# Making the low part of streamed weights for two halves of a block by one instruction

## The reference, cut to what matters

```python
def sqrelu_mlp(h, w_up, w_down):
    u = jax.nn.relu(h @ w_up)
    return (u * u) @ w_down

def reference(x, ...):
    for layer in range(DEPTH):                       # DEPTH = 2
        h = rmsnorm(x, norm_mix_w[layer])
        y = hybrid_mixer(h, ...) if layer % 2 == 0 else swa_sink_attention(h, ...)
        x = x + y
        h = rmsnorm(x, norm_mlp_w[layer])
        x = x + sqrelu_mlp(h, mlp_w_up[layer], mlp_w_down[layer])
    return rmsnorm(x, final_norm_w)
```

## Time and profile before

| what | value |
|---|---|
| median of three runs | 2006.84 us (2005.88 to 2007.82) |
| profiled execution, its span from the first to the last instruction | 2005.7 us |
| TensorE busy | 1997.1 us, 9161 products |
| VectorE busy | 1450.5 us, 2028 instructions |
| ScalarE busy | 1027.4 us, 1360 instructions |
| low parts on VectorE (L854) | 708 of 128x1024, 858.9 us |
| transfers of weights on SyncE's queue | 57.0% of the 16 engines' span |

### The profile page before, as it was taken

How to read it: one execution, slowest core, us unless ns; L and a number is a source line. 1 busy time by engine, 2 the same in 40 slices (tenths; PEclk the granted TensorE clock), 3 DMA queues, 4 the chain that set the end, 5 groups by cost and what they waited for, 6 DMA issues and landing times.

```text
span 2005.7 us, 24710 instructions
## 1 busy us (share of the span) xinstructions
PE 1997.1 (100%) x9161; PEld 1653.1 (82%) x9161; DVE 1450.5 (72%) x2028; ACT 1027.4 (51%) x1360; POOL 45.1 (2%) x55
## 2 busy tenths in 40 slices
PE   9999999999999999999999999999999999999998
PEld 8888888888888888888888878888888888888887
DVE  6777778987558647755889887988548756854875
ACT  6665665455345435434545566555435444534554
POOL 1110110000000000000000000000000000000000
PEclk9999999999999999999999999999999999999999
DMA  8556546556555565555655544565565555565563
GB/s 304 181 176 214 170 167 211 189 189 209 191 189 192 198 195 185 193 195 181 210 189 189 169 162 163 181 203 194 194 197 193 192 190 187 187 209 189 189 201 113
DMA packets 191756, 382.48 MB, mean 191 GB/s; under 512 B 6328, under 2 KB 7616, under 8 KB 191552
## 3 DMA queue, kind: packets, MB, share of 16 engines
q1 hardware_dynamic: 190288, 377.51, 57.0%
q0 software_dynamic: 1216, 3.88, 0.6%
q10 hardware_dynamic: 176, 0.07, 0.0%
HBM read 379.34 MB, written 2.10 MB: 190 GB/s over the span
## 4 chain that ended last, share of the span: by engine, by line
PE 98%; DVE 1%; issue 0%; ACT 0%; DMA 0%; ACTq 0%
PE acc L1215 31%; PE acc L1217 31%; PE acc L1216 31%; DVE area L1052 1%; PE bank L1305 0%; PE bank L1382 0%; PE bank L1406 0%; PE bank L1392 0%; DVE w_lo L854 0%; PE acc L1244 0%; PE acc L1248 0%; PE acc L1252 0%; PE bank L1347 0%; PE bank L1336 0%; PE bank L1337 0%
## 5 line engine op out<-in xcount | busy, mean ns | idle before, releaser
L854 DVE TENSOR_TENSOR w_lo<-raw,w_hi 128x1024 fp32r<-128x1024 f32 x708 | 858.9, 1223 | 497.8 <-ACT w_hi L622 494.9
L622 ACT ACTIVATE w_hi<-raw 128x1024 fp32r<-128x1024 f32 x708 | 743.5, 1060 | 772.3 <-PE acc L1217 771.0
L1215 PE MATMUL acc<-w_hi,a_hi 128*128 128x512 f32 x1552 | 607.1, 391 | 0.0
L1217 PE MATMUL acc<-w_hi,a_lo 128*128 128x512 f32 x1552 | 604.1, 389 | 0.0
L1216 PE MATMUL acc<-w_lo,a_hi 128*128 128x512 f32 x1552 | 604.0, 389 | 0.0
L1215 PE MATMUL acc<-w_hi,b_hi 128*128 128x512 f32 x1264 | 492.3, 389 | 0.0
L1216 PE MATMUL acc<-w_lo,b_hi 128*128 128x512 f32 x1264 | 491.8, 389 | 0.0
L1217 PE MATMUL acc<-w_hi,b_lo 128*128 128x512 f32 x1264 | 491.7, 389 | 0.0
L1215 PEld LDWEIGHTS acc<-w_hi,a_hi 128*128 128x128 f32 x1552 | 291.4, 188 | 61.2 <-issue 0.9
L1217 PEld LDWEIGHTS acc<-w_hi,a_lo 128*128 128x128 f32 x1552 | 291.3, 188 | 60.9
L1216 PEld LDWEIGHTS acc<-w_lo,a_hi 128*128 128x128 f32 x1552 | 291.4, 188 | 60.0
(11 more groups left out here) (204 smaller groups left out, 602.1 us busy)
## 6 DMA issues: line engine op xcount, KB each, us to landing
raw<-in_mlp_w_up SPq DMA_DIRECT2D x128, 1024.0 KB, 5.3
raw<-in_mlp_w_down SPq DMA_DIRECT2D x128, 1024.0 KB, 5.1
raw<-in_hyb_w_in SPq DMA_DIRECT2D x44, 1024.0 KB, 5.2
raw<-in_attn_w_qkv SPq DMA_DIRECT2D x20, 1024.0 KB, 5.2
raw<-in_hyb_w_out SPq DMA_DIRECT2D x16, 1024.0 KB, 5.1
raw<-in_attn_w_out SPq DMA_DIRECT2D x16, 1024.0 KB, 5.0
raw<-in_hyb_w_in SPq DMA_DIRECT2D x5, 512.0 KB, 9.5
out_y<-x SPq DMA_DIRECT2D x4, 512.0 KB, 3.0
```

Of the source, the lines that this page charges most:

```text
L622: nc.scalar.activation(w_hi[:, h % RING], raw[:, h // 2, 2 * (h % 2):2 * (h % 2) + 2, :], ACT.Copy).then_inc(hi_ready, 1)
L854: nc.vector.tensor_tensor(w_lo[:, h % RING], raw[:, h // 2, 2 * (h % 2):2 * (h % 2) + 2, :], w_hi[:, h % RING].bitcast(F32), ALU.subtract) ...
L1215: nc.tensor.matmul(a, xh, wh, start=first, stop=False)
L1217: ins = nc.tensor.matmul(a, xl, wh, start=False, stop=last)
```

## The change

`cut_lo` does nothing at an even half. At an odd half it waits for that half's high part, which comes after that of the even half, and makes the low parts of both by one instruction over 128x2048 elements; the semaphore rises by 2. The raw weights of the two halves lie side by side in one place, and their two places of the ring too.

```diff
@@ cut_lo, on VectorE @@
                 h = n % HALVES
                 if slot.b * HALVES + n >= NBLK * HALVES:
                     return
+                if h % 2 == 0:
+                    return
+                to = slice(h % RING - 1, h % RING + 1)
                 dve.wait_ge(hi_ready, slot.halves(n + 1))
-                nc.vector.tensor_tensor(w_lo[:, h % RING], raw[:, h // 2, 2 * (h % 2):2 * (h % 2) + 2, :],
-                                        w_hi[:, h % RING].bitcast(F32), ALU.subtract).then_inc(lo_ready, 1)
+                nc.vector.tensor_tensor(w_lo[:, to].rearrange("p h e n -> p (h e) n"), raw[:, h // 2],
+                                        w_hi[:, to].rearrange("p h e n -> p (h e) n").bitcast(F32),
+                                        ALU.subtract).then_inc(lo_ready, 2)
```

## The result

The changed kernel takes 2098.88 us (median of four runs, 2098.01 to 2100.95) against 2007.07 us of the kernel before in the same session: 1.0462 times as long, with a 95% interval of 1.0447 to 1.0477. The forecast was 2079 us; the time lies 0.9 us above the top of the range.

What follows compares the result with a forecast made beforehand. TensorE, busy 1997.1 of 2005.7 us, was taken to bound the kernel. Waits at the listed places summed to 72.0 us, making the span 2077.7; with the median 1.1 higher, the forecast was 2079 us, range 2050 to 2098.

Steps and rivals of the forecast that it cites:

- TensorE bounds the kernel: Whole kernel: TensorE busy 1997.1 of 2005.7 us, so savings on other engines bring at most 8.6 us.
- The price of the long instruction: Each low part of 128x2048 on VectorE: 2.29 us, with bounds of 1.23 and 2.46.
- The places: Waits placed behind `up`, `res`, `q`, `k`, `aq`, `v`, `g`, in slots 55 and 56, at start and end: 72.0 us.
- the ring sets the earliest start of a pair: Any pair: its high part starts only after half k-3; with nothing else to do, ready 3.58 us later, due at 5.44.
- No waits behind `down`: Slots behind `down`: no TensorE waits at pairs expected; seeing some would be a sign of being wrong.
- What a wait costs beyond its length: Every TensorE wait: 0.17 us added for restart, signal and load, with bounds of 0 and 0.31.
- the lateness of the pair: Behind `up` and similar, 36 places: pair ends at 11.30 against 10.88 us, late by 0.42.
- TensorE's clock falls: Behind six waits of 3 to 5 us: nine products at 1.2 GHz pace, 1.8 us each wait; 2090 us, chance 0.10.
- a granted clock under full after the long waits: TensorE after long waits: a profile sign that the forecast is wrong; no size given.
- Waits breed waits: Even pairs with slack run late because a late pair delays loads and evacuations: above 2098 us, chance 0.08.
- Behind `v`: Decay of retention scores stands behind the pair 5.4/5.5: 1.43 us late with the restart, twice.
- half 56.0: One slot after slot 55: what is late there is late again, 1.55 us.

Runs made afterwards that it cites:

- the ring of eight: Changed kernel with rings of high and low parts holding eight halves instead of four, two low-part buffers left out: 2036.47 us, ratio 1.0155.
- the pairs first: Changed kernel with each pair placed on VectorE ahead of the odd tick's own work instead of behind it: 2219.42 us, ratio 1.1062.

## Why the prediction was wrong by 20 us

**Right.** That TensorE bounds the kernel and VectorE's saving is worth nothing (shown by the pairs behind `down`). The Trainium skill (VectorE: DVE Perf Modes, the section on the TRN2 errata) advises large tiles to pay the fixed latency less often; the trace agrees on VectorE, busy 43.7 us less, and the kernel's time rose all the same. The price of the long instruction, 2.294 us against 2.29. The places, and what stands ahead of each: four transposes, twelve, two pairs against 10.88 us. That the ring sets the earliest start of a pair, from which that arithmetic begins, is shown by the ring of eight. No waits behind `down` appeared.

**The step that failed: "What a wait costs beyond its length".** It gave each wait 0.17 and let everything go on at 0.227 us a product from there. Behind the long waits and at the start TensorE did not go on at that pace: 14.2 us, most of the miss, and the next part is on them. Behind the short waits the term was nearly right in its sum, and not in its parts. It was made of 0.08 from the earlier trace rows and of 0.09 for signal and load, which no row shows. And that row isn't one of a restart: a small product runs just ahead of half 0.6, which starts at 28.65 (TensorE's timeline in the kernel before):

```profile
28.56 0.28 PE L1471 MATMUL bank<-ident,vec_rows 72*128 72x72 f32 x1
```

In the change, 51 of the 58 waits have no slow half behind them. In 38 of these the half begins 0.05 behind the pair's end and takes 0.14 longer in the mean; in the other 13 it begins 0.15 behind and takes 0.08 longer. That is 0.20 for 0.17, some 2 us in all.

**A second term was too small: the lateness of the pair.** Behind `up` the pair ends 0.52 late, not 0.42: 36 times 0.10, 3.5 us. That the late start came out at 0.57 for 0.58 is luck, 0.10 more here against 0.12 less in the signal. Of the 0.10, 0.07 lies between a high part's end and its low part's start, for which the sum had 0.03. That holds in the kernel before (ScalarE, then VectorE, in slot 19):

```profile
454.44 1.06 ACT L622 ACTIVATE w_hi<-raw 128x1024 fp32r<-128x1024 f32 x1
455.53 1.23 DVE L854 TENSOR_TENSOR w_lo<-raw,w_hi 128x1024 fp32r<-128x1024 f32 x1 [1.92 <-ACT w_hi L622]
```

There the low part starts 0.03 behind the high part's end, as in all 382 cases in which VectorE had been idle for over 0.1 us; the pair in slot 19 starts 0.10 behind it (507.18 + 1.06, then 508.34), as do 243 of 245 such pairs. With two instructions it is 0.03 again. Whether the length makes it, the signal of 2 or something else, was not tried.

**The rival that was put aside came true: "TensorE's clock falls".** It had 0.10, because TensorE would be idle "but a few us at a time, between long stretches of work". That argument has no row behind it, and it is wrong; the prediction had named a granted clock under full after the long waits as a sign of being wrong, and that sign came. Behind each of the six waits of 3.3 to 4.8 us in the changed kernel, and behind that of 1.71 at the start, a half ran slow, with the granted clock at or near half in the windows. They cost 1.73 + 2.31 + 1.52 + 1.72 in slots 3, 4, 9 and 10, 2.66 + 1.30 at the start and 2.57 + 0.40 in slot 55, 14.2 us together. The rival assumed nine products, or 1.8 us each, at six places, 11 us: the right size. The added products show that idleness is the cause at the four places where they stood. The Trainium skill (TensorE: Matmul & The Clock Gate, section HAM oscillation) describes this for waits on data; the trace agrees here for waits on another engine.

**"Waits breed waits"** has its number, above 2098, by 0.9 us, but not its mechanism: slots with slack, those behind `down`, run as before.

**Sizes.** Behind `v` 2.02 was measured for 1.43. Of the 0.6, 0.42 is the pair 5.4/5.5 itself. The timeline of VectorE, then of GpSimd:

```profile
156.56 2.71 DVE L857 TENSOR_TENSOR w_lo<-raw,w_hi 128x2048 fp32r<-128x2048 f32 x1 [1.50 <-ACT w_hi L622]
...
156.39 0.74 POOL L598 TENSOR_TENSOR area<-area 128x256 f32<-128x256 f32 x1
```

Of 354 low parts this one and its twin in slot 11 are the only ones over 2.4 us, and both begin 0.17 us into that GpSimd instruction. In the kernel of two instructions the two low parts at this place take 2.86 us beside the same GpSimd instruction, where two in a row take 2.35 in the kernel before. That the two hinder each other is likely by this, and was not tried by itself. At half 56.0 0.75 came for 1.55, and half 0.1 started 1.8 us earlier than before, both in the other direction; the second is a difference between executions.

The late starts thus make 72 us, as forecast, and what follows them some 20. With the 5 us measured for the two short terms and the rival's 11 to 14 us in the sum, it would have come out at 2095 to 2098.

## What to carry to other kernels

An engine that is never waited for can be made cheaper at no gain, and merging its instructions makes the first result as late as the last: before merging, write down when each part is due, and count the work that stands ahead of the merged one. A wait of the bounding engine costs more than its length: add the restart, and where it is some us long, the slow work behind it, from a row of either. Before moving an instruction to an earlier place in its queue, follow what then stands behind it to the engine that waits for that; here this turned a loss of 92 us into one of 213.

## What the runs showed of the hardware

Even a half-clock stretch that costs 2.3 us cannot be seen in the page's clock row; windows of 3 to 4 us show it. How often a stop was followed by a slow half (over 1 us lost), with the long waits of the recurrent slots: after 4.8 us in 8 of 8 (the change and the kernel with pairs at the long waits alone), after 3.7 us in 3 of 4 (two instructions), after 3.06 us in 1 of 4 (ring of eight); after 0.57 to 2.03 us in 0 of 53 in the change, the start left out. It isn't a matter of length alone. With two instructions, a stop of 1.86 us in slot 11 was followed by a stretch at half clock, and one of 3.57 us in slot 10 was not. The kernel with the pairs first, at a ring of four, has waits of 2.29 us with a slow half behind them (1.30 lost at half 26.2) and without (0.13 at half 34.2). What decides was not found. Work of no use, put into the four waits of 4.8 us, paid for itself.
